# Reordering ScalarE's root, TensorE's write-out and VectorE's first dot products at the start of an expert stage

## The reference, cut to what matters

```
h = h + concatenate([y_mla, y_diff], axis=-1) @ w_out        # y_diff is normed by head before
xc = rms_norm(h, ffn_norm)
q = (xc @ w_query).reshape(128, 8, 2, 128)                    # 8 heads, two halves
s = einsum('chpd,hpnd->chpn', q, sub_keys)
s1, i1 = top_k(s[:, :, 0], 16); s2, i2 = top_k(s[:, :, 1], 16)
best, flat = top_k(s1 + s2 over all pairs, 16)                # the pair search
experts = i1[flat // 16] * 128 + i2[flat % 16]; g = softmax(best)
act = gelu(einsum('cd,chkd->chk', xc, u[experts]))            # the dot products
h = h + einsum('chk,chkd->cd', g * act, v[experts])
```

## Time and profile before

| what | us |
|---|---|
| median of 3 runs | 1554.97 |
| lowest and highest of them | 1554.42, 1567.65 |
| the profiled execution, its own time | 1558.44 |
| its span in the profile | 1556.70 |
| PE busy | 1218.5 (78%) |
| DVE busy | 1044.4 (67%) |
| POOL busy | 589.6 (38%) |
| ACT busy | 429.6 (28%) |
| bytes read, mean rate | 433.44 MB, 280 GB/s |

### The profile page before, as it was taken

One profiled execution on the slowest core, in us unless ns is written; L12 is line 12 of the kernel. 1 busy time (PEld: TensorE's weight loads), 2 busy tenths in 40 slices (PEclk: granted clock), 3 DMA queues, 4 the chain that ended last, 5 costly groups with the idle time before them and its releaser, 6 DMA issues.

```text
span 1556.7 us, 17603 instructions
## 1 busy us (share of the span) xinstructions
PE 1218.5 (78%) x6509; PEld 883.1 (57%) x6509; DVE 1044.4 (67%) x1929; ACT 429.6 (28%) x745; POOL 589.6 (38%) x644
## 2 busy tenths in 40 slices
PE   6998867775776654656566456999999999999997
PEld 3555643532443321222222123989999999899997
DVE  5877577868546775686655555667778888755546
ACT  1156212111101110111110102333335655344332
POOL 4140164657667566767777665001001000000000
PEclk9999888997888877878786787999999999999999
DMA  9816297989999899989999999677849666444562
GB/s 343 333 39 227 69 353 285 349 334 375 337 378 366 321 343 401 400 320 375 346 373 399 354 354 383 217 244 272 286 157 325 206 212 195 145 135 163 178 208 86
DMA packets 179997, 435.46 MB, mean 280 GB/s; under 512 B 13913, under 2 KB 84642, under 8 KB 179926
## 3 DMA queue, kind: packets, MB, share of 16 engines
q0 software_dynamic: 84384, 306.26, 51.6%
q1 hardware_dynamic: 94404, 126.16, 24.3%
q10 hardware_dynamic: 1138, 2.12, 0.4%
HBM read 433.44 MB, written 2.14 MB: 280 GB/s over the span
## 4 chain that ended last, share of the span: by engine, by line
PE 43%; POOL 19%; DVE 15%; issue 11%; another core or an unknown queue 6%; DMA 4%; ACT 3%; SPq 0%; DVEq 0%; POOLq 0%; ACTq 0%
POOL arena L804 14%; PE quad L1562 14%; PE quad_a L1668 7%; PE quad_a L1576 6%; PE quad_a L1235 4%; POOL ring L804 3%; DVE arena L2240 3%; DVE ring L2240 2%; PE quad L1321 2%; DMA ring<-in_ffn_w_gu_dram 2%; PE quad_a L1733 1%; POOL row L804 1%; DVE hx L2257 1%; PE quad_a L1748 1%
## 5 line engine op out<-in xcount | busy, mean ns | idle before, releaser
L1512 PE MATMUL quad_a<-arena 128*128 128x512 f32 x368 | 189.6, 675 | 157.4 <-DMA arena<-in_peer_v_dram,arena 92.3
L1512 PEld LDWEIGHTS quad_a<-arena 128*128 128x128 f32 x368 | 78.2, 220 | 268.1 <-issue 241.7
L804 POOL DMA_INDIRECT arena<-in_peer_v_dram,arena x174 | 170.6, 981 | 84.9 <-issue 54.7
L1562 PE MATMUL quad<-u_hi,w_hi 128*128 128x256 f32 x704 | 198.8, 282 | 2.5 <-DVE u_lo L2134 2.5
L1562 PE MATMUL quad<-u_lo,w_hi 128*128 128x256 f32 x704 | 198.7, 282 | 0.0
L1562 PE MATMUL quad<-u_hi,w_lo 128*128 128x256 f32 x704 | 198.6, 282 | 0.0
L2073 DVE TENSOR_TENSOR w_lo<-ring,w_hi 128x2048 fp32r<-128x2048 f32 x66 | 150.8, 2290 | 63.7 <-ACT w_hi L1015 63.4
L804 POOL DMA_INDIRECT arena<-in_peer_u_dram,arena x156 | 159.4, 1022 | 78.3 <-issue 48.7
L1512 PE MATMUL quad<-arena 128*128 128x512 f32 x184 | 104.2, 708 | 72.2 <-DMA arena<-in_peer_v_dram,arena 37.9
L2240 DVE CUSTOM_DVE_ANT_0 arena<-arena,quad_a 128x1024 f32<-128x1024 f32 x120 | 143.0, 1219 | 16.4 <-DMA arena<-in_peer_u_dram,arena 14.0
L1009 ACT ACTIVATE arena<-ident,arena 128x128 f32<-128x128 f32 x188 | 59.1, 389 | 323.1 <-issue 158.4
(11 more groups left out here) (402 smaller groups left out, 2508.6 us busy)
## 6 DMA issues: line engine op xcount, KB each, us to landing
ring<-in_ffn_w_gu_dram SPq DMA_DIRECT2D x44, 1024.0 KB, 9.4
arena<-in_w_ada_dram POOLq DMA_DIRECT2D x60, 512.0 KB, 7.0
ring<-in_ffn_w_down_dram SPq DMA_DIRECT2D x22, 1024.0 KB, 5.1
ring<-in_w_mix_in_dram SPq DMA_DIRECT2D x20, 1024.0 KB, 6.3
arena<-in_peer_w_query_dram SPq DMA_DIRECT2D x4, 2048.0 KB, 11.9
arena<-in_w_in_dram SPq DMA_DIRECT2D x3, 2048.0 KB, 31.1
ring<-in_w_ada_dram POOLq DMA_DIRECT2D x12, 512.0 KB, 9.4
arena<-in_w_out_dram SPq DMA_DIRECT2D x2, 2048.0 KB, 11.7
```

The lines of the kernel that those rows point to most:

```text
L804: gp.indirect_dma_start(out=rows_of(n), out_offset=None, in_=t["peer_" + kind][0], in_offset=bass.IndirectOffsetOnAxis(ap=expert[tt][:, sl ...
L1512: last = te.matmul(sum_side[tt][:, cols], diag[:, i % DIAGS], rows_of(n)[:, cols], start=(slot == pe_slots[tt][0]), stop=(slot == pe_slots ...
L1562: last = te.matmul(psum[c][:, w * SEQ:(w + 1) * SEQ], weight[a][:, k, (c % 2) * P:(c % 2 + 1) * P], (u_hi, u_lo)[b][:, k], start=(k == 0 a ...
```

## The change

On ACT four things. The copies of step 5's turned probabilities come after the root of tile 0's second norm in place of before it. The copy of `hn[0]` into PSUM comes ahead of head 1's `spread_rows` and `soft`. `first_modulation` comes behind the first GELU. On PE the first four chunks of both halves of tile 1's write-out are multiplied ahead of the transpose of its differential half and right behind it, as for tile 0, and all three jobs of the modulation come behind the write-out. On DVE head 1's key search comes ahead of `y_turned(1)`, and head 1's pair search behind the dot products of group 0 and tile 1's two additions. No instruction is added or taken away.

```
--- before.py
+++ after.py
@@ -949,7 +949,7 @@
                     evac_heads(*LATER[i])
                 if i == 6:
                     root(("subln", 0))
-                if i >= 2:
+                if 2 <= i < 7:
                     turned_out(i - 2)
             def evac_half(what, half):
                 segs = slice(2 * half, 2 * half + 2)
@@ -959,6 +959,7 @@
             k, cols, _ = norm_at["h1", 0]
             sc_e.wait_ge(sums.sem, k + 1)
             roots.mark(ac.activation(rstd[:, cols], stats[:, cols], ACT.Sqrt, bias=h1_bias, scale=1.0 / D))
+            turned_out(5)
             evac_half("pq", 0)
             evac_half("ps", 0)
             turned_out(6)
@@ -986,11 +987,10 @@
             evac_half("pq", 1)
             evac_half("ps", 1)
             root(("subln", 1))
-            first_modulation()
+            sc_e.wait_ge(d_free.sem, len(d_jobs))
+            hn_in_psum.mark(ac.activation(hn_side[0], hn[0], ACT.Copy))
             spread_rows(1)
             soft(1)
-            sc_e.wait_ge(d_free.sem, len(d_jobs))
-            hn_in_psum.mark(ac.activation(hn_side[0], hn[0], ACT.Copy))
             def gelu_group(group):
                 tt, first = group // GROUPS, group % GROUPS * GB
                 used(sc_e, set_of("u", tt, first + GB - 1))
@@ -1043,6 +1043,7 @@
             for group in range(QT * GROUPS):
                 gelu_group(group)
                 if group == 0:
+                    first_modulation()
                     evac_query("pq", 0, 1)
                     evac_query("ps", 0, 1)
                 if group == QUERY1_AT:
@@ -1321,10 +1322,6 @@
                     last = te.matmul(bank[:, :], yT[tt][:, k], wo_half[n][:, k], start=(k == 0), stop=(k == KD - 1))
                 return last
 
-            def write_out(n, tt):
-                d_bank(("wo", n, tt))
-                d_full.mark(write_rows(n, tt, range(KD)))
-
             def turn_keys(n):
                 pe.wait_ge(ld_keys, 16)
                 bank = a_bank(("keysT", n))
@@ -1476,15 +1473,18 @@
             values(7)
             first_query(1)
             first_scores(1)
-            pe.wait_ge(ada_used.sem, ada_count(0, False))
-            a_full.mark(over_partitions(a_bank(("ada", "columns")), 0, "columns"))
+            d_bank(("wo", 0, 1))
+            write_rows(0, 1, range(KD // 2))
             pe.wait_ge(y_ready.sem, 2)
             turn_y(1)
-            for job in (0, 1):
-                a_full.mark(over_partitions(a_bank(("ada", job)), 0, job))
+            d_bank(("wo", 1, 1))
+            write_rows(1, 1, range(KD // 2))
             pe.wait_ge(d_free.sem, d_at["yT", 1] + 1)
             for n in range(2):
-                write_out(n, 1)
+                d_full.mark(write_rows(n, 1, range(KD // 2, KD)))
+            pe.wait_ge(ada_used.sem, ada_count(0, False))
+            for job in ADA_JOBS:
+                a_full.mark(over_partitions(a_bank(("ada", job)), 0, job))
             query(0, 1)
             key_scores(0, 1)
 
@@ -2271,14 +2271,14 @@
             y_squared(1)
             normalize(0)
             y_normed(1)
+            first_keys(1)
             y_turned(1)
-            first_keys(1)
-            top_pairs(1)
             ve.wait_ge(hn_ready.sem, 2)
             dot_rows(0, range(0, GB - 1), hn[0])
             written_out(0, 1)
             dot_rows(0, range(GB - 1, GB), hn[0])
             written_out(1, 1)
+            top_pairs(1)
 
             for group in range(QT * GROUPS + 1):
                 tt, first = group // GROUPS, group % GROUPS * GB
```

## The result

| what | before | after |
|---|---|---|
| median of 11 runs each on one chip | 1563.58 | 1551.77 |
| lowest to highest of them | 1554.42 to 1569.64 | 1543.75 to 1560.23 |
| ratio after to before, 95% interval | | 0.9923 [0.9898, 0.9948] |
| the profiled execution, its own time | 1558.44 | 1543.75 |
| its span | 1556.70 | 1541.6 |

A forecast was written before the change was run, and what follows sets the result against it. It took transfers to bound the expert stage (DMA share 0.96). Earlier marks shifted the end of ACT's long wait by 8.8 us, the middle of 7.6 and 9.9; off the median 1554.97 that gave 1546.2, range 1539 to 1557.

The forecast's parts named there:

- Step 1, root: ACT, tile 0's second norm: root ahead of eight copies brings the first gather 6.3 us earlier, bounds 3.6 and 6.4.
- Step 2, write-out: PE, tile 1: write-out ends 14.8 us earlier, 6.3 from the root, 8.1 from sums behind it, 0.4 from the clock.
- Step 3, dots: DVE, head 1: first dot from 202.86 to 191.1, next dots 9.0 us earlier; 19th gather waits 5.4 us, cost 0.
- first dry stretch: Transfers running dry for 3.60 us at 203.0 in the kernel before; forecast to go.
- Step 4, the long stop: ACT's 20.04 us wait before the first query-column copy, read as code fetch: same copy, ending 8.8 us earlier.
- both bounds: End of ACT's long wait: 226.8 with the transfers, 9.9 us earlier, or 229.1 at its old length, 7.6 earlier.
- the stage behind carries it: Expert stage after the wait: paced by transfers, it was to keep the whole 8.8 us lead to the end.
- The stop is gone: Rival, chance 0.14: ACT's long wait is bad luck of timing and vanishes, 15.8 us less, 1539.
- second dry stretch: Transfers running dry for 5.90 us at 239.7 in the kernel before; forecast to remain, some 9 us earlier.
- Given back: Rival, chance 0.19: the expert stage's own waits soak up the lead, time 1553 to 1555.
- Slower: Rival, chance 0.09: ACT meets a second long wait at the three modulation copies, price 14 to 20 us, 1563.
- three conditions for being wrong: First gather under 3 us earlier, ACT's long wait ending after 236, or lead at 945 us smaller than at 250.

The follow-up runs named there:

- undo_root_timed: Changed kernel with step 5's probability copies put back ahead of tile 0's second root; same kernel executed twice under two names; ratio to before 0.9942 over 12 executions.
- root_only: Kernel before with only the eight copies of turned probabilities moved behind the root of tile 0's second norm; ratio to before 0.9955 over eleven executions.
- experiment 4: Changed kernel with DVE's old order put back, first dots behind head 1's pair search, profiled twice; ratio to before 0.991 over four executions.
- after_again: The changed kernel profiled once more, nothing altered; own time 1546.10 us.
- pad3: Changed kernel with three tiny ACT copies added in idle time ahead of tile 0's second root; own time 1538.42 us.
- pad32: Changed kernel with 32 tiny ACT copies added in idle time ahead of tile 0's second root; ratio to before 0.9917 over four executions.
- undo_dots_timed: Second execution of the changed kernel with DVE's first dots put back behind head 1's pair search; own time 1549.11 us.

## Why the prediction was right, and where it was not

**Step 1, root: right.** Measured values come first, forecast ones in brackets. Root done at 164.17 (163.5), in an execution that reached the seam 0.65 later; the clock kept up, columns from 167.47 at 3.84 us, first gather at 183.72 (183.2). The value was 6.3; `undo_root_timed` and `root_only` measure 6.5 over the same distance. Both halves of the reasoning hold: 4 us of idle and 2 of clock.

**Step 2, write-out: right.** It ends at 198.97 (198.6), and the next query columns end at 214.7 (214.0). The covers held: the scaling of the turned half is done at 191.50, ahead of PE, which has it at about 192.0 (188.50 and a third of 10.47). The wide sums ran at a granted clock of 0.50 from 203.0. The same is in the kernel before: 0.50 from 195 to 199, where the same sums stood.

**Step 3, dots: right at each mark, with less behind it than it seems.** First dot 191.41 (191.1), eighth gather 192.97 (192.5), next dots 209.45 (210.4), 19th gather 210.95 (211.9), no first dry stretch. The 19th gather waited 1.28 us and not 5.4, because POOL's own pace was slower than the step has it. What the step does not say is that its worth hangs from the stop: with it, the 29th and the 32nd gather are held by other things, and without it experiment 4 has some 4 us at the 32nd gather. In the time it was not measurable.

**Step 4, the long stop: near in size, wrong in its reading.** The forecast gain was 8.8, between 7.6 and 9.9, with the end of the stop at 227 to 229; it ended at 225.35, 11.3 earlier than before and outside both bounds. It began 8.9 earlier (206.64 + 1.08 against 216.66) and was 2.4 shorter, 17.63 for 20.04; the forecast had taken one bound with the old length and the middle between the two. That the long stop was met at all was partly luck: of the two executions of the changed kernel one has it in full. The step says that ACT stood still "though the columns were ready at 220.5", and reads this as a fetch of ACT's code. Both fall: PE's count for the columns went up at 236.67, and ACT left 0.02 us later. That it should be met at the same copy was right in place, and not as a prediction of length: two executions of one program had 17.63 and 8.97 + 4.46, `undo_root` had 17.62 and `undo_root_timed` none, and moving the code did not move it. The Trainium skill's rule on code fetched a block ahead and mostly hidden (Runtime: NRT & Kernel Launch, Instruction fetch mechanics) is neither shown nor refuted by this: the two instruction queues in part 3 of the profile moved one packet of 0.01 MB between 200 and 230 us in the changed kernel, and one was moved in just that part of the seam in executions with the stop and without. For ACT the question does not arise, since its copy began as soon as its semaphore allowed.

**The sum.** 8.8 was forecast, and a median gain of 11.8 measured (8 to 16). The seam's lead of 11.35 at the 32nd gather agrees with this, if a stage paced by transfers carries it to the end. It has two halves: the columns' matmuls end 5.8 us earlier by PE's rows (214.72 for 220.49), which is the change's doing, and PE's count for them was late by 10.6 and not by 16.2, which differs from execution to execution and so is in part luck. That "the stage behind carries it" agrees in the mean with `root_only`, which turned 6.4 at the seam into 7 at the end. It is wrong for one execution: from the 32nd gather to the 512th the kernel before took 700.7 and 702.2 us, the changed one 695.0 and 703.3. The profiled pair's 14.7 is the seam's 11.4 with some 3 of such scatter.

**The rivals.** *The stop is gone* was priced at 15.8 us and the forecast at 8.8. At the seam that price was about right: in the three executions of the changed code with the stop short or away (`after_again`, `pad3`, `pad32`) the 32nd gather came 15.1 to 18.1 earlier than before, where it was 11.4 with the stop. Whether it is carried is not settled. At the 512th gather these three stand at 934.1 to 939.5 and the one with the stop at 934.0, but the latter had the fastest stretch of all fourteen behind the seam (695.0); against the 951.1 and 954.0 of the kernel before, the three are 11.6 to 19.9 ahead. The ratios of 0.9917 and 0.9923 do not decide it either, since only the profiled executions tell whether the stop was there. Why the lead at the seam is not larger is in a row of POOL's timeline of `pad32`, with its windows:

```profile
235.25 1.94 POOL L804 DMA_INDIRECT ring<-in_peer_u_dram,arena  x1 [7.41 <-DVE hx L2259]
```

```profile
228.00:234.00 6.00, 1.56 (x4) 0.38 (x2) 3.43 (x25) 2.61 (x4) 0.00 (x0) 1.00 0.96 382
234.00:239.00 5.00, 0.00 (x0) 0.00 (x0) 4.85 (x8) 0.27 (x2) 3.14 (x3) 0.58 0.23 52
```

The second dry stretch has a second cause behind the first: DVE's add, which stands behind its key search. With the stop gone it is this that lets the transfers run dry here (share 0.23), and in `undo_dots_timed` the same row has 7.56. *Given back* didn't happen: the lead at the 512th gather was 17.1 in the pair, and the medians keep 11.8. *Slower*, a second stop at the modulation's copies, didn't either: they run at 206.57 to 207.7, with full transfers, without a wait. None of the three conditions for being wrong was met; of the signs, the end of the stop was missed by 1.7 us.

**Which edit the time is from.** By the ratios: the root 0.0045 when added alone and 0.0019 when taken away last; the write-out 0.0027 when taken away; the dots and ScalarE's order -0.0013 and -0.0009, which is nothing. All intervals are about 0.003 to either side, and a difference of two ratios is less certain still. So the root's part of the 0.0077 is shown, the rest is not assigned, and the write-out is its likeliest source.

**What stays open.** Why PE's count comes late, and why PE starts its matmuls one by one in experiment 4. Both belong to PE, to the query columns and their scores, and to full transfers, so they may be one thing. A starved supply of PE's instructions would fit, with the end of the one-by-one matmuls as the transfers run dry, but this was not shown: no run took the profile's own records away, or the load of the transfers, with the same code.

## What to carry to other kernels

Look for a small operation with a long wait behind work that isn't urgent, on the engine that the next stage hangs from: here one square root of 1.6 us with its table load held up PE, and with it the clock. Before a wait is laid to the engine that waits, look up when its semaphore went up. Compare marks only between executions in the same case, with the stop or without it. Removing a visible wait is worth time only if the next wait hangs from it; before an edit is priced, follow the engine that issues the transfers to its next three waits. In a stage paced by transfers one profiled pair can differ by 12 us with no edit between, so rate edits of a few us by repeated times, and marks by their distance from the last mark that the edit can't touch.

## What the runs showed of the hardware

- A wait of 3.6 us on PE costs its clock too: the same 32 matmuls took 5.81, 6.73, 5.88 and 5.79 us behind it in four executions, and 3.84 in all nine without it.
- The granted clock fell with PE busy without a break, behind the one-column sums. In the changed kernel these stand from 198.8 to 202.8, and the clock is 1.00 to 201, 0.72 from 201 to 203, and 0.50 from 203.0 to 206.6. In the kernel before they stand from 190.5 to 195.4, and the clock is 0.76 from 190 to 195 and 0.50 from 195 to 199. The gathers are not what lowers it: under full transfers it is 1.00 over the write-out, from 190 to 196 in the changed kernel.
- PE's count for a group of matmuls came up to 17.9 us after the end in PE's rows, and ACT stood still for up to 20 us waiting for it; in other executions PE started single matmuls 1.4 or 2.1 us apart. Both came with full transfers, and in some executions of a program and not in others.
- Over the stage, ACT's waits of releaser "remote" on L831 rose with no harm to the time, for the earlier trace rows now reads:

```profile
ACT arena L831 <- remote: 106.1, 9, 19.9
```
